# Each adaLN row from four 32-column tiles of TensorE instead of one column of it

## The reference, cut to what matters

```python
mod = jnp.dot(jax.nn.silu(c), w_ada[l]) + b_ada[l]                 # (1, 1024) x (1024, 6144)
sh1, sc1, gt1, sh2, sc2, gt2 = [m[:, None, :] for m in jnp.split(mod, 6, axis=-1)]
h = rmsnorm(x, g_pre_mix[l]) * (1.0 + sc1) + sh1
...
y = jnp.dot(jnp.concatenate([y_m, y_a], axis=-1), w_out[l])        # mLSTM and sparse attention
x = x + gt1 * rmsnorm(y, g_post_mix[l])
h2 = rmsnorm(x, g_pre_ffn[l]) * (1.0 + sc2) + sh2
y2 = moe(h2, ...)                                                  # 32 experts
x = x + gt2 * rmsnorm(y2, g_post_ffn[l])
...
mod = jax.nn.silu(c) @ ada_w[l] + ada_b[l]                         # second layer: (1, 1024) x (1024, 3072)
```

## Time and profile before

| | |
|---|---|
| time, median of 3 runs | 2424.37 us (2421.81 to 2426.69) |
| the profiled execution: span from first to last instruction | 2420.5 us |
| what lies around the span | not given apart; the median of the runs is 3.9 us above the span |
| PE busy | 2190.2 us, 90% of the span |
| block 1 / 2 / 3 / 4 | ends at 68.4 / 168 / 326.4 / 382.3 us |

### The profile page before, as it was taken

The page is one execution under the profiler, slowest core; times in us unless marked ns, Lnnn a source line. Parts: engine busy times, 40 slices in busy tenths (PEclk is TensorE's granted clock), DMA queues, the critical chain, the costliest instruction groups (busy, mean ns, idle before and its releaser), DMA issues. The chain is left out here.

```text
span 2420.5 us, 29654 instructions
## 1 busy us (share of the span) xinstructions
PE 2190.2 (90%) x10208; PEld 1677.8 (69%) x10208; DVE 1563.1 (65%) x1413; ACT 1202.0 (50%) x1252; POOL 559.9 (23%) x147
## 2 busy tenths in 40 slices
PE   7889985999999999999999999999998699889998
PEld 4675364777777777777777777777777368766777
DVE  1314205798898898898898898898898344144401
ACT  1112304666666666666666666666665214622210
POOL 0000001323323323323323323323323002411000
PEclk8998995999999999999999999999999799989999
DMA  9743503888888778888888888878876532313220
GB/s 330 191 148 139 209 1 97 273 278 278 275 278 280 270 281 279 271 281 279 270 282 279 273 279 280 273 278 277 274 280 208 202 140 105 138 46 129 105 103 20
DMA packets 252653, 525.24 MB, mean 217 GB/s; under 512 B 27442, under 2 KB 34714, under 8 KB 252474
## 3 DMA queue, kind: packets, MB, share of 16 engines
q1 hardware_dynamic: 240538, 521.40, 62.9%
q10 hardware_dynamic: 12064, 3.15, 0.9%
HBM read 522.88 MB, written 1.06 MB: 216 GB/s over the span
## 5 line engine op out<-in xcount | busy, mean ns | idle before, releaser
L1203 DVE TENSOR_TENSOR low<-ring_low,high 128x2048 fp32r<-128x2048 f32 x288 | 851.1, 2963 | 160.8 <-ACT high L1341 160.5
L1341 ACT ACTIVATE high<-ring_low 128x2048 fp32r<-128x2048 f32 x384 | 727.1, 1911 | 72.5 <-PE ps L1285 51.4
L1203 POOL TENSOR_TENSOR low<-ring_low,high 128x2048 fp32r<-128x2048 f32 x96 | 485.1, 5053 | 966.9 <-ACT high L1341 953.4
L1285 PE MATMUL ps<-high,xh 128*128 128x512 f32 x1024 | 298.4, 413 | 0.0
L1285 PE MATMUL ps<-high,xl 128*128 128x512 f32 x1024 | 281.1, 396 | 0.0
L1285 PE MATMUL ps<-low,xh 128*128 128x512 f32 x1024 | 281.0, 396 | 0.0
L1285 PEld LDWEIGHTS ps<-low,xh 128*128 128x128 f32 x1024 | 192.8, 188 | 46.7
L1285 PEld LDWEIGHTS ps<-high,xl 128*128 128x128 f32 x1024 | 190.6, 188 | 43.5
L1285 PEld LDWEIGHTS ps<-high,xh 128*128 128x128 f32 x1024 | 186.5, 189 | 40.9 <-issue 0.3
L1350 ACT ACTIVATE sg<-gl 128x512 f32<-128x512 f32 x64 | 40.5, 633 | 294.9 <-DVE gl L1418 294.9
L1421 DVE SCALAR_TENSOR_TENSOR li<-li,gl 128x512 f32<-128x512 f32 x64 | 144.4, 2256 | 8.2
(11 more groups left out here) (470 smaller groups left out, 2985.6 us busy)
## 6 DMA issues: line engine op xcount, KB each, us to landing
ring_low<-in_w_up_dram SPq DMA_DIRECT2D x512, 512.0 KB, 5.8
ring_low<-in_w_down_dram SPq DMA_DIRECT2D x128, 1024.0 KB, 6.3
second_ring<-in_w_in_dram SPq DMA_DIRECT2D x11, 2048.0 KB, 8.0
ring_low<-in_w_in_dram SPq DMA_DIRECT2D x10, 2048.0 KB, 8.5
first_ring<-in_w_ada_dram SPq DMA_DIRECT2D x7, 2048.0 KB, 8.1
ring_low<-in_w_ada_dram SPq DMA_DIRECT2D x5, 2048.0 KB, 8.3
first_ring<-in_ada_w_dram SPq DMA_DIRECT2D x4, 2048.0 KB, 8.2
first_ring<-in_w_in_dram SPq DMA_DIRECT2D x3, 2048.0 KB, 20.6
```

The lines of the kernel that those rows point to most:

```text
L1203: eng.tensor_tensor(low[:, sl, :], raw[:, sl, :], high[:, sl, :].bitcast(F32), ALU.subtract)\
L1285: mm = pe.matmul(ps[:, bank + c, :], x[:, 2 * kp + q, :], w[:, q * D + c * 512:q * D + (c + 1) * 512], start=(first and i == 0 and q == 0) ...
L1341: act.activation(high[:, sl, :], raw[:, sl, :], ACT.Copy).then_inc(s("w_high"), 1)
```

## The change

A row is now made by four tiles of 32 columns each. Tile q (columns 32q to 32q+31) takes input tiles k = 2q and 2q+1, with `silc[:, k]` repeated over its 32 columns, and writes its partial row, 32 times the same, to partitions 32q to 32q+31. The whole bank is thus one row's. ACT copies all 128 partitions, SP sends the four partial rows with four DMAs, and the sum over the four is made by the matmul that turns rows into columns: against a 0/1 matrix `C_SUM4` for the 14 rows of block 3, against `C_PICK` (1 in partitions 0, 32, 64 and 96) for the four rows of block 1. `mrow` has two places now instead of four.

```diff
-        def mod_row(pe, n, which, m, bank):
-
-            q = 32 * (m % 4)
-            for k in range(KT):
-                mm = pe.matmul(ps[q:q + 1, bank, :], silc[:, which, k:k + 1], slots[n % len(slots)][:, k, :],
-                               start=(k == 0), stop=(k == KT - 1))
+        def mod_row(pe, n, which, bank):
+
+            for kk in range(2):
+                for q in range(4):
+                    k = 2 * q + kk
+                    mm = pe.matmul(ps[32 * q:32 * q + 32, bank, :], silc[:, which, k:k + 1].to_broadcast([P, 32]),
+                                   slots[n % len(slots)][:, k, :], start=(kk == 0), stop=(kk == 1))
             mm.then_inc(sm("slab_used"), 1)
 
         def mod_row_copy(act, n, m, bank):
-            q = 32 * (m % 4)
+            i = m - 4
             act.wait_ge(sm("slab_used"), n + 1)
-            if m >= 8:
-                act.wait_ge(sm(f"mod_rows_in{m % 4}"), 16 * (m // 4 - 1))
-            S.done(act, act.activation(mrow[q:q + 1, :], ps[q:q + 1, bank, :], ACT.Copy), sm("mod_row_ready"))
-
-        def mod_row_send(sp, m, at):
-
+            if i >= 2:
+                act.wait_ge(sm(f"mod_rows_in{i % 2}"), 64 * (i // 2))
+            S.done(act, act.activation(mrow[:, i % 2, :], ps[:, bank, :], ACT.Copy), sm("mod_row_ready"))
+
+        def mod_row_send(sp, m):
+            i = m - 4
             sp.wait_ge(sm("mod_row_ready"), m + 1)
-            q = 32 * (m % 4)
-            sp.dma_start(mrows[at:at + 4, :], mrow[q:q + 1, :].rearrange("a (j p) -> a j p", p=P))\
-                .then_inc(sm(f"mod_rows_in{m % 4}"), 16)
+            for q in range(4):
+                at = 16 * (i % 7) + 4 * q
+                sp.dma_start(mrows[at:at + 4, i // 7, :], mrow[32 * q:32 * q + 1, i % 2, :].rearrange("a (j p) -> a j p", p=P))\
+                    .then_inc(sm(f"mod_rows_in{i % 2}"), 16)
...
-                        S.done(act, act.activation(first_rows[:, n * 512:(n + 1) * 512], ps[32 * n:32 * n + 1, 5, :], ACT.Copy),
+                        S.done(act, act.activation(first_rows[:, n * 512:(n + 1) * 512], ps[:, n, :], ACT.Copy),
                                sm("mod_row_ready"))
...
-                        mod_row(pe, n, 0, n, 5)
+                        mod_row(pe, n, 0, n)
...
-                            if m >= 8:
-                                pe.wait_ge(sm("mod_row_ready"), m - 3)
-                            mod_row(pe, n, 0 if m < 12 else 1, m, 3)
+                            if m > 4:
+                                pe.wait_ge(sm("mod_row_ready"), m)
+                            mod_row(pe, n, 0 if m < 12 else 1, 3)
...
-                    pe.transpose(ps[:, 6, 0:56], mrows[:], cst[0:56, C_ID:C_ID + 56]).then_inc(sm("mod_turned"), 1)
+                    for half in range(2):
+                        mm = pe.matmul(ps[:, 6, 28 * half:28 * half + 28], mrows[:, half, :],
+                                       cst[0:112, C_SUM4:C_SUM4 + 28], start=True, stop=True)
+                    mm.then_inc(sm("mod_turned"), 1)
```

More of the change, by code:

```diff
@@ L71 @@
 C_FLIP = C_LATER + P
-C_W = C_FLIP + P
+C_PICK = C_FLIP + P
+C_SUM4 = C_PICK + 1
+C_W = C_SUM4 + 28
 K_RV = 0
@@ L96, in shape_constants @@
         c[:, C_VALC + t * NCMP:C_VALC + (t + 1) * NCMP] = ok
+    c[:, C_PICK] = np.arange(P) % 32 == 0
+    for r in range(7 * 16):
+        c[r, C_SUM4 + 4 * (r // 16) + r % 4] = 1
     c[:96, C_SEL3:C_SEL3 + NE] = np.arange(96)[:, None] % 32 == np.arange(NE)[None, :]
@@ L203, in two_layers @@
         gain = sb("gain", [P, KT])
-        mrow = sb("mrow", [P, 512])
-        mrows = sb("mrows", [56, P])
         idn = cst[:, C_ID:C_ID + P]
@@ L334, in two_layers @@
             xtok = sb("xtok", [P, TT, D], at=pa)
-            first_rows = sb("first_rows", [1, 4 * 512], at=pa)
+            first_rows = sb("first_rows", [P, 4 * 512], at=pa)
             c32 = sb("c32", [NBUCKET, K_W], at=pa)
@@ L410, in _ @@
                         for k in range(4 * n, 4 * n + 4):
-                            mm = pe.matmul(ps[:, 4, k:k + 1], first_rows[:, k * P:(k + 1) * P], cst[0:1, C_ONES:C_ONES + 1],
+                            mm = pe.matmul(ps[:, 4, k:k + 1], first_rows[:, k * P:(k + 1) * P], cst[:, C_PICK:C_PICK + 1],
                                            start=True, stop=True)
@@ L449, in two_layers @@
         qkT = sb("qkT", [P, 2 * MH, SEQ], at=att)
+        mrow = sb("mrow", [P, 2, 512], at=att)
+        mrows = sb("mrows", [7 * 16, 2, P], at=att)
         vm = sb("vm", [P, TT, MH * MD], at=att)
@@ L622, in _ @@
                             load_slab(sp, n, SLABS1[n])
-                        mod_row_send(sp, m, 4 * (m - 4))
+                        mod_row_send(sp, m)
                 @block.scalar
@@ L800, in _ @@
                     mods(4)
-                    for q in range(4):
-                        pe.wait_ge(sm(f"mod_rows_in{q}"), 16 * len(range(4 + q, 18, 4)))
+                    for b in range(2):
+                        pe.wait_ge(sm(f"mod_rows_in{b}"), 64 * 7)
                     pe.wait_ge(sm("pt_ready"), len(ROUNDS))
-                    pe.transpose(ps[:, 6, 0:56], mrows[:], cst[0:56, C_ID:C_ID + 56]).then_inc(sm("mod_turned"), 1)
+                    for half in range(2):
+                        mm = pe.matmul(ps[:, 6, 28 * half:28 * half + 28], mrows[:, half, :],
+                                       cst[0:112, C_SUM4:C_SUM4 + 28], start=True, stop=True)
+                    mm.then_inc(sm("mod_turned"), 1)
                     for sl, (par, hh) in enumerate(SLOTLIST):
```

## The result

| | before | changed kernel |
|---|---|---|
| time, median of 6 runs each | 2423.76 us (2420.41 to 2426.69) | 2411.82 us (2402.45 to 2417.78) |
| ratio, 95% interval | 1 | 0.995, 0.9933 to 0.9967 |
| profiled execution: span | 2420.5 us | 2411.5 us |

The changed kernel is 12 us (0.5%) faster: the forecast side, inside its range (2392 to 2418), and 8 us short of the forecast of 2404. By time alone the first rival (2416) lies nearer, and the median is just outside the bounds of the forecast case (2399 to 2410); what decides between the two is the trace. The other thing to explain is the spread: the executions of the changed kernel lie 15 us apart, those of before 6 (10 over the 19 runs of a later batch).

What follows compares the result with a forecast made beforehand. The prediction took DMA transfers to bound block 1 and PE's rows between attention chain steps to bound block 3. Block 1's 0, block 3's -21.7 and the clock's +1.7 made -20.0 us on 2420.5; plus 3.9, 2404 us, range 2392 to 2418.

Steps and rivals of the forecast that it cites:

- the first rival: Four-tile rows: records start in order, so a row takes 8 distances, 3.43 us; -8, 2416 us; chance 0.10.
- the forecast case: Whole kernel: 2404 us, with bounds 2399 to 2410; chance 0.72.
- The price of a row: Four-tile row on PE: four tiles overlap, 1.8 us taken; without any overlap 6.86.
- the second: Four-tile rows: one tile's weight loads can't run beside another's matmul; row 6.86 us, +31, 2455 us; chance 0.06.
- Block 1: 0: Block 1: rows end some 15 us earlier but gain nothing, since the full DMA queue sets the block's end.
- The third rival: Block 1 isn't held by the queue, so its 15 us would come too: 2389 us; chance 0.05.
- The walk through block 3: Block 3's rows between attention chain steps: gains and new waits, in all -21.7 us by the last turn.
- row 10, L787: Block 3, after the first turn of 24 records, taken as 3.9 us: -3.6, in all -15.0.
- rows 14 to 17, last turn: End of block 3: -8.3, in all -21.7; row 15's copy waits for row 13's sends behind slab 26.
- The clock term, "+1.7": Ahead of the last turn: PE idles about 4.4 us, half speed for 3.4 us costs 1.7.
- The bounds (-25 to -14): Whole kernel: -25 without low clock or slab 26 wait (2399); -14 with 1.2 GHz wherever there's a gap (2410).
- "The gain is given back": Later sends or copies wait for more than seen, behind slabs or ACT's exponentials: 2420 us, no change; chance 0.07.

Runs made afterwards that it cites:

- one tile: Changed kernel with all eight input tiles in one 32-column tile, handshake, four sends and two places of `mrow` kept; 2456.83 us.
- the kernel with block 1 alone: The kernel before with four-tile rows in block 1 only, block 3 as before; 2424.62 us, ratio 1.0001.
- second profile: Unaltered changed kernel run again, 8 runs with median 2413.67 us; the profiled execution was the fastest, 2401.56 us.
- filling the wait: Changed kernel plus five unused float32 matmuls between row 17 and the turn, where PE waited for the sends; 2401.58 us.
- moving it: Changed kernel with the turn of the 14 rows and DVE's bias sums moved behind the attention output; 2399.61 us.
- the kernel with sends ahead of slabs: Changed kernel with five unused matmuls before the last turn, plus rows 12 and 13 sent before slabs 25 and 26 are issued; 2405.28 us.
- the one with two banks and the turn last: Changed kernel with the turn behind the attention output, plus odd rows from row 9 on in PSUM bank 2; 2389.0 us.
- the two repetitions: Changed kernel run again unaltered, twice; 2409.06 us and 2413.67 us.
- the long rows with added idle time: The kernel before with three more 2 KB DMAs ahead of row 17's send, lengthening PE's wait; 2427.44 us, again 2426.62 us.

## Why the prediction was right, and where its size was off

The mechanism came as predicted: the row price, block 1, and the waits that it named in block 3. The size did not, and one term of the sum, the clock, is why. That the median still fell into the range is in part due to the range's width, which had to reach past the first rival.

**The price of a row** was right: 1.73 measured, 1.8 taken. The Trainium skill (TensorE: Matmul & The Clock Gate, Part 3) lets weight loads overlap with matmuls in flight only for other row groups; the four tiles use the same rows, and the rows of block 1 show four of them at full speed. The measurement decides against the rule for this case. The first rival (2416) would have shown rows of 3.43 at 2.4 GHz and isn't there; the second is what one tile measured.

**Block 1: 0** was right, shown by the trace after (67.98) and by the kernel with block 1 alone (1.0001). The third rival falls with it.

**The walk through block 3**, step by step, as times on the span's clock. The first column of measurements is the changed kernel's profile, in which the block's row 4 started 0.9 later than before; the second is the profile at 2401.56 us.

| step | forecast | measured | measured, second profile |
|---|---|---|---|
| rows 4 to 6, L741 | 210.7 | 213.00 | 210.88 |
| row 7, L749 | 214.4 | 216.34 | 214.33 |
| rows 8 and 9, first L768 | 238.4 | 240.33 | 238.32 |
| row 10, L787 | 244.5 | 244.95 | 242.99 |
| rows 11 to 13, second L768 | 267.2 | 267.42 | 265.45 |
| rows 14 to 17, last turn | 286.3 | 288.19 | 286.13 |
| idle time ahead of the turn | 4.4 | 4.27 | 4.27 |

The end fits better than the steps. In the second profile L787 and the second L768 come 1.5 to 1.8 us before their forecast, in the main because the first turn's 24 records took 2.8 us and not 3.9, and rows 14 to 17 then took 20.7 us where 19.1 were forecast. The last turn took 0.95 in the changed kernel's profile (288.19 to 289.14) in place of 0.16, so 0.8 more and not 0.3. The reasons hold. Row 15's copy waited 4.48 for a DMA, the send of row 13. SP issued slab 26 at 268.21, ahead of that send (from 268.70 on), which landed by 278.4; that the slab held it back is read from this order. ACT's waits for sends over block 3 (us in total, times, longest) are new, and row 15's copy is the longest of them:

```profile
ACT mrow L290 <- DMA mrows<-mrow: 6.5, 3, 4.5
278.48 0.60 ACT L290 ACTIVATE mrow<-ps 128x512 f32<-128x512 f32 x1 [4.48 <-DMA mrows<-mrow]
```

**The clock term, "+1.7", is the one that was mis-sized.** It measured +12.3 in the profiled execution (28.5 against 16.2 for the same work) and 1.3 in the second profile (17.5 against 16.2), whose block 4 starts 20.1 us earlier than before and whose span is 20.7 shorter (2399.8; the forecast's sum was 2400.5). With the 12.3 the sum is: -20.0 + (12.3 - 1.7) = -9.4, and the span fell by 9.0. That they meet is partly luck, for two smaller differences cancel: the output started 2.4 us later than forecast (-19.3 in place of -21.7), and block 4 gained 1.7: it began at 0.68 of the clock before (326 to 330) and at 1.00 after (319 to 323), and the difference of -6.9 at its start is -8.6 at 382 (L1066 at 373.69 instead of 382.31). The forecast of 2404 is near the time of the executions where the low level ends early in the output (2401.56 and 2405.27); the median execution is some 7 us above it. The price came from a stretch of 3.4 us in the earlier trace rows, and what failed is the step from there: "the lower level lasted 3.4 us" was taken for its length here too. Behind long rows that held in three profiles. Behind short rows it held in one of three: the others have 27 us, and 17 us that took in rows 16 and 17, where it cost 3.4 us ahead of the output (3.64 instead of 1.92 for each). The bounds (-25 to -14) counted rows and turns at 1.2 GHz, but never the output.

Two small things in the sums: of the 3.9 us between span and median only 1.8 lie around the span (in every run: 2422.3 against 2420.5), the rest is that the profiled execution was faster than the median. And the rivals' chances add up to 0.87 for faster and 0.07 for no change, where the text has 0.88 and 0.05.

That the shortfall goes when PE doesn't idle ahead of the output is shown twice, by filling the wait and by moving it: 2401.58 and 2399.61, below the forecast, with spreads of 2.6 and 1.5 us over 4 runs each. That the whole spread of the changed kernel comes from there is not shown: only three of its 20 executions have a profile, two of them differ by 3.7 us from ahead of the output, and the kernel with sends ahead of slabs, filled too, still spread 6.5, the one with two banks and the turn last 7.7. Why the low level lasts 27 us in one execution, 17 in another and 3.4 in a third stays open. The Trainium skill (the same page, Part 1) says of a kernel's start that the number of matmuls at the lower level differs between runs of the same kernel; at the start of this one no run here was compared for it.

"The gain is given back" (2420) named later sends and copies. Part of the gain was given back, but by the clock and not by them.

## What to carry to other kernels

Before pricing a faster stage, ask of each barrier and each chain step which engine comes last: here 16 us less of PE in block 1 were worth nothing, and 14 rows between chain steps all of the gain. A split that takes a whole PSUM bank adds a handshake for every result; a second bank for every other row gave 10.6 us (2399.61 to 2389.0), nearly as much again as the change had gained (12). Where TensorE has become the engine that waits, don't let it idle right ahead of a dense stage: put behind that stage what needs late transfers, and don't price a low clock there by one observed stretch: the three profiles of one kernel had 3.4, 17 and 27 us.

## What the runs showed of the hardware, unexpected

- The granted clock stayed at 1.2 GHz for 27 us (288.1 to 315.4) while PE was busy all the time with matmuls of 64 columns. The durations agree with the record: `ps<-qkT,vcm` took 1.11 instead of 0.64. In five other profiles of this or nearly this program (the two repetitions, the long rows with added idle time twice, the one tile) it came back within 3.4 us of the output's start. A busy PE at the low level isn't new with the change: in the kernel before the granted clock was 0.50 from 180 to 190, at the start of block 3, with PE busy all the time.

```profile
180.00:185.00 5.00, 5.00 (x25) 5.00 (x25) 0.33 (x2) 0.00 (x0) 0.00 (x0) 0.50 0.00 0
```

- Adding 5 us of useless matmuls saved 7 us or more of the median time.
- Four column tiles with 128 partitions each, float32, run at the full rate of one: 16 records in 1.73 us, against 6.9 in one tile.
- Copies waited 4.4 to 4.5 us for small sends that were issued right behind a 2 MB load, and sending two rows ahead of the loads only handed that wait to the next rows.
